# A two-block network on one core: the last expert tile added by one-hot products in PSUM, attention heads split from PSUM, one head scaled on GpSimd

## The chip, the cores and the metric

The kernel runs on one core of a Trainium2 chip. The metric is the device time of one execution in microseconds (us). Engines are named as the profile names them: PE is TensorE's matmul side and PEld its weight load, DVE is VectorE, ACT is ScalarE, POOL is GpSimd, and SP is SyncE, which here only starts transfers.

## The reference

One sequence of 512 tokens with 1024 channels goes through two layers of a first block (recurrence, latent attention, a convolutional feed-forward part) and then two layers of a second block. The change touches the second block alone. What it computes in each layer, cut to what matters:

```python
y_hy = hyena_mixer(...)                       # long convolution, here by DFT products
s = einsum(q, k); pr = softmax(s)             # 4 heads, two softmaxes each
o = einsum(pr[:, 0] - lam * pr[:, 1], v)
y_att = rms_norm_2(o, subln_g) * (1 - lam_init)
y_pool = pool_mixer(...)
h = layer_norm_2(ALPHA * h + concatenate([y_hy, y_att, y_pool]) @ w_out)
act = silu(h @ w1[e]) * (h @ w3[e]) * gate    # two of 16 experts for each token
y_moe = sum over e of act @ w2[e]
h = layer_norm_2(ALPHA * h + y_moe + y_ple)
```

## The kernel before

Activations are kept with channels on the 128 partitions and 512 tokens along the free axis, as 8 chunks. A large f32 product is made of three fp32r products, high by high, low by high and high by low (`three`, L257 to L259); so each operand is first split into a rounded high part and the rest. POOL splits the streamed weights (L180 makes the high part, L182 the low part), ACT and DVE split activations and the experts' weights.

The order of the work in the second block is written out by hand for each engine and held together by semaphores. Each engine runs its own list in order, so an instruction that waits holds up all that is behind it.

**The attention loop** has 16 steps n, four query blocks for each of four heads. In a step PE makes the scores for step n+2 (L2097), turns the weighted difference of the two softmaxes of step n (`turn`, L2110) and multiplies it with v (`weigh`, L2119). ACT takes the exponentials (L2450), copies the turned block (L2458) and scales the head's output (L2466). DVE takes the row maximum for step n+2 (L2777) and makes the difference for step n+1 (`difference`, L2784 to L2786). Between these, all three work on the hyena part: PE makes its projections and DFT products, ACT starts the short convolution of a tile (`hy_tile`, L2395), DVE ends it (`hy_taps`, L2666 and L2667), and `hyena_out` (L2826 on) writes the two output chunks at steps 13 and 14. Four blocks after a head began, DVE scales it by the reciprocal root (`norm_out`, L2806 and L2807, for heads 0, 1 and 2 at steps 4, 8 and 12), and PE turns it at steps 6, 10 and 14 (`turn_out`, L2127). At these steps DVE copies the turned head from PSUM to `tmp` (`att_take`, L2813), which sets `ot_taken`; PE's `turn` of steps 7, 11 and 15 waits for that, since both use PSUM bank 4. The split of `tmp` into `mix_h` and `mix_l` (L2641, L2642) comes at steps 7, 11 and 14. The last head is split from PSUM itself (L2875, L2876). POOL meanwhile forms the spectra's product, copies the inverse DFT's tables, and splits the first output weights, the third of them into a pair of buffers of its own (`split_apart`).

**The expert tiles** come after routing. There are 23 tiles of 128 rows: one for each expert, and 7 spare ones for experts with more than 128 tokens. POOL gathers a tile's rows by index (L1882). PE turns them (`turn_rows`, L2288) into two PSUM banks; ACT rounds them to `xgT_h` (L2575), DVE makes `xgT_l` (L3054). The expert's first weights, 2 MB, come in four parts, each rounded on ACT (L2569) and its rest taken on DVE (L3042). PE makes 24 products of 512 columns (`expert_up`, `ps<-ew_h,xgT_h` and its two like), ACT and DVE make the gated activation (L2597, L3097), PE turns it (L2326), DVE copies it (`hidden_evac`, L3060), and PE multiplies it by the 1 MB second weights (`expert_down`, L2344, plain f32). ACT and DVE each copy one half of the result (L2583, L3067), and POOL adds the rows to `yrows` in HBM by index (`scatter_rows`, L1913). DVE's list within a tile begins with the weights of the next one. For the first tile it is: three parts of tile 1's weights, a step of the residual (L3089), both halves of tile 1's rows, the activation, the fourth part.

**The end of a layer** starts when both of the last scatters have landed: SP loads `yrows` as four blocks of 128 tokens (L1792), PE has turned the residual z into the eight PSUM banks (L2364), DVE adds the two and sums each row (`pick_rows`, L3109), ACT squares (L2609), DVE and POOL normalise, and PE turns the four blocks back (L2373), once the last `pick_rows` has left the banks free. Scale and shift on ACT and DVE follow, and then the store or the next layer.

## Time and profile before

| what | value |
|---|---|
| runs | 2795.28, 2794.57 and 2798.91 us; median 2795.28 us |
| profiled execution | 2797.76 us, its span 2795.9 us |
| mean granted TensorE clock | 0.982 of full speed |
| PE busy | 2707.6 us, 97% of the span |
| DVE busy | 1746.7 us, 62% |
| POOL busy | 1601.3 us, 57% |
| ACT busy | 1096.7 us, 39% |

Times inside a run are us from the start of the span. The second block's layers have their attention loops at about 1740 to 1850 and 2310 to 2420, their expert tiles at 1956 to 2200 and 2527 to 2771, and their ends at 2200 to 2218 and 2771 to 2796. What stands in brackets behind a row, `[1.16 <-DVE tmp L2813]`, is the idle time of the engine just ahead of the row and what ended it.

### The profile page before, as it was taken

The numbers are of one execution on the slowest core, as the hardware profiler recorded it, in microseconds if no ns is written. First come the engines' busy times: TensorE is split into PE (matmuls) and PEld (weight loads), VectorE is DVE, ScalarE is ACT, GpSimd is POOL, SyncE is SP. The second block draws the span as 40 slices with busy tenths as digits, with TensorE's granted clock in tenths as the row PEclk, the third lists the DMA queues.
The fourth block names the chain that finished last, engine by engine and source line by source line (L and its number), as shares of the span: only waits on it lengthen the run. The fifth ranks groups of instructions, "written<-read, shape, count | busy, mean of one in ns | idle before, by whom it ended". The sixth has DMA issues, their size and how long they took to land. (4 is left out here: it accounts for less than half of the span.)

```text
span 2795.9 us, 35382 instructions
## 1 busy us (share of the span) xinstructions
PE 2707.6 (97%) x12410; PEld 2117.4 (76%) x12410; DVE 1746.7 (62%) x2544; ACT 1096.7 (39%) x1895; POOL 1601.3 (57%) x987
## 2 busy tenths in 40 slices
PE   8999999999999999999999999989999799899997
PEld 6777778888887777788888877778776577777775
DVE  6787755443137878654442148876877497877774
ACT  3744323222025544332221032544655315445553
POOL 5754466666677643476666765565236455662263
PEclk9999999999999999999999979999999999999999
DMA  4222222333332311223333322136995222257951
GB/s 153 83 76 61 63 88 76 98 98 98 95 94 79 96 61 61 68 80 96 96 98 106 97 74 91 54 106 230 336 353 160 82 88 69 91 202 288 347 173 61
DMA packets 89050, 337.16 MB, mean 121 GB/s; under 512 B 21584, under 2 KB 24400, under 8 KB 79568
## 3 DMA queue, kind: packets, MB, share of 16 engines
q1 hardware_dynamic: 66592, 298.02, 31.6%
q0 software_dynamic: 19296, 26.29, 3.6%
q10 hardware_dynamic: 3024, 11.01, 1.0%
q8 instruction: 87, 1.43, 0.2%
q14 instruction: 51, 0.42, 0.0%
HBM read 366.67 MB, written 34.60 MB: 144 GB/s over the span
## 5 line engine op out<-in xcount | busy, mean ns | idle before, releaser
L182 POOL TENSOR_TENSOR wl<-ring,wh 128x1024 fp32r<-128x1024 f32 x319 | 785.5, 2462 | 26.6
L180 POOL TENSOR_SCALAR wh<-ring 128x1024 fp32r<-128x1024 f32 x319 | 349.0, 1094 | 754.8 <-PE ps L259 529.3
L257 PE MATMUL ps<-xh,wh 128*128 128x512 f32 x1608 | 640.3, 398 | 15.3 <-DVE xl L1245 10.8
L258 PE MATMUL ps<-xl,wh 128*128 128x512 f32 x1608 | 628.6, 391 | 0.0
L259 PE MATMUL ps<-xh,wl 128*128 128x512 f32 x1608 | 628.5, 391 | 0.0
L257 PEld LDWEIGHTS ps<-xh,wh 128*128 128x128 f32 x1608 | 303.1, 189 | 96.0 <-issue 12.6
L259 PEld LDWEIGHTS ps<-xh,wl 128*128 128x128 f32 x1608 | 303.3, 189 | 64.6
L258 PEld LDWEIGHTS ps<-xl,wh 128*128 128x128 f32 x1608 | 303.5, 189 | 61.8 <-issue 1.0
L1487 DVE SCALAR_TENSOR_TENSOR taps<-ps,par,taps 128x511 f32<-128x511 f32 x192 | 143.8, 749 | 232.6 <-ACT taps L1219 217.7
L3042 DVE TENSOR_TENSOR ew_l<-ew,ew_h 128x1024 fp32r<-128x1024 f32 x184 | 213.3, 1217 | 4.4 <-ACT ew_h L2569 4.4
L2569 ACT ACTIVATE ew_h<-ew 128x1024 fp32r<-128x1024 f32 x184 | 180.4, 1050 | 10.6 <-DMA ew<-in_eu 7.2
L1219 ACT ACTIVATE taps<-ps,par 128x512 f32<-128x512 f32 x96 | 74.5, 778 | 271.8 <-PE ps L259 271.6
L2344 PE MATMUL ps<-ew,hactT 128*128 128x512 f32 x368 | 167.0, 597 | 4.4 <-DVE hactT L3060 4.4
L257 PE MATMUL ps<-ew_h,xgT_h 128*128 128x512 f32 x368 | 161.2, 438 | 4.6 <-issue 4.6
L379 DVE TENSOR_TENSOR z<-z,ps 128x512 f32<-128x512 f32 x44 | 30.2, 687 | 213.1 <-PE ps L259 212.7
L441 ACT ACTIVATE sqb<-z 128x512 f32<-128x512 f32 x48 | 30.3, 632 | 335.6 <-DVE z L379 247.4
L257 PE MATMUL ps<-hid_h,wh 128*128 128x512 f32 x384 | 149.9, 390 | 0.0
L259 PE MATMUL ps<-hid_h,wl 128*128 128x512 f32 x384 | 149.4, 389 | 0.0
L258 PE MATMUL ps<-hid_l,wh 128*128 128x512 f32 x384 | 149.4, 389 | 0.0
L259 PE MATMUL ps<-ew_h,xgT_l 128*128 128x512 f32 x368 | 144.8, 393 | 0.0
L258 PE MATMUL ps<-ew_l,xgT_h 128*128 128x512 f32 x368 | 144.5, 393 | 0.0
L1882 POOL DMA_INDIRECT xg<-xrows,idx x46 | 48.3, 1050 | 138.7 <-PE ps L2288 122.7
(537 smaller groups left out, 5329.1 us busy)
## 6 DMA issues: line engine op xcount, KB each, us to landing
ring<-in_w SPq DMA_DIRECT2D x343, 512.0 KB, 3.6
ew<-in_eu SPq DMA_DIRECT2D x32, 2048.0 KB, 11.4
ew<-in_ed SPq DMA_DIRECT2D x32, 1024.0 KB, 11.9
xrows<-xr ACTq DMA_DIRECT2D x8, 512.0 KB, 2.7
yrows<-xr ACTq DMA_DIRECT2D x8, 512.0 KB, 3.6
yg<-yrows SPq DMA_DIRECT2D x8, 512.0 KB, 5.1
z<-in_x SPq DMA_DIRECT2D x4, 512.0 KB, 6.0
out<-z SPq DMA_DIRECT2D x8, 256.0 KB, 2.9
```

The source lines that it names most:

```text
L180: nc.gpsimd.tensor_scalar(hi, raw, 1.0, 0.0, ALU.mult, ALU.add).then_inc(sem["w_hi"], 1)
L182: nc.gpsimd.tensor_tensor(lo, raw, hi, ALU.subtract).then_inc(sem["w_split"], 1)
L257: nc.tensor.matmul(out, wh, xh, start=first, stop=False, **kw)
L258: nc.tensor.matmul(out, wh, xl, start=False, stop=False, **kw)
L259: return nc.tensor.matmul(out, wl, xh, start=False, stop=last, **kw)
L441: nc.scalar.activation(sqb[:, m % 2, :], z[:, m, :], ACT.Square).then_inc(sem["sq_part"], 1)
L1219: nc.scalar.activation(taps[:, j % 2, half, :], ps[:, 2 * j + half, :], ACT.Identity, scale=col(layer, "ffw", f + (2 * 2 * FC + half * FC) ...
L1487: ins = V.scalar_tensor_tensor(out, ps[:, 2 * j + half, 0:S - s], col(layer, "ffw", f + ((2 - s) * 2 * FC + half * FC)), out, ALU.mult, AL ...
L1882: nc.gpsimd.indirect_dma_start(xg[:, j % 2, :], None, xrows[:, :], bass.IndirectOffsetOnAxis(ap=idx[:, held(j):held(j) + 1], axis=0), boun ...
L2344: mm = T.matmul(ps[:, 5 + half, :], hactT[:, f, :], ew[:, b, a_:a_ + S], start=(f == 0), stop=(f == EC - 1))
L2569: A(ew_h[:, n % HI_SLOTS, :], ew[:, b, u * D:u * D + D], ACT.Copy).then_inc(sem["e_hi"], 1)
L3042: V.tensor_tensor(ew_l[:, b, u * D:u * D + D], ew[:, b, u * D:u * D + D], ew_h[:, n % HI_SLOTS, :], ALU.subtract).then_inc(sem["e_lo"], 1)
```

## The change

In the attention loop `att_take` now writes `mix_h` and `mix_l` straight from PSUM (two instructions on DVE where there were one at this place and two later), the buffer `tmp` and the semaphore `ot_taken` are gone, and PE's `turn` of steps 7, 11 and 15 waits for `att_done`. The scaling of head 2 goes from DVE to POOL, ahead of its split of the first output weights; DVE keeps the reciprocal and signals `o_root`. POOL's `split_apart` waits until the 16th difference is made. ACT starts the last hyena tile ahead of the exponentials of step 13 and not behind them.

Around the first expert tiles, ACT brings the table for the Silu up front and rounds the second half of tile 1's rows before tile 0's activation. DVE takes the two halves of tile 1's rows between the parts of tile 1's weights.

At a layer's end, tile 22 is no longer scattered. The SP loads wait for the 22 other scatters only. DVE keeps the last tile's row indices, turns them into four one-hot matrices `last_hot` (128 by 512 in all) at tile 8, and ACT and DVE split the last tile's result into `last_h` and `last_l`. PE turns z with matmuls that leave the PSUM groups open and adds `last_hot` by `last_h` and by `last_l` in each of the eight banks: 16 fp32r products of 512 columns more in each layer.

```diff
+        last_hot = at_("last_hot", 180, [P, 4, P], F32R)
+        last_h = at_("last_h", 164, [P, D], F32R)
+        last_l = at_("last_l", 176, [P, D], F32R)
...
+        TAP_LAST = 11
         HALF_AT = {7: (4, 0), 8: (4, 1), 9: (5, 0), 10: (5, 1)}
         FOLD_AT = 8
+        POOL_HEAD = 2
         NORM_AT = (2,)
         STACK_AT = 1
-        SPLIT_AT = (7, 11, 14)
...
-                    sp.wait_ge(sem["y_out0"], at("y_out0", 16 * turns_of(TILES, 0, 2)))
-                    sp.wait_ge(sem["y_out1"], at("y_out1", 16 * turns_of(TILES, 1, 2)))
+                    sp.wait_ge(sem["y_out0"], at("y_out0", 16 * turns_of(TILES - 1, 0, 2)))
+                    sp.wait_ge(sem["y_out1"], at("y_out1", 16 * turns_of(TILES - 1, 1, 2)))
...
+                    g.wait_ge(sem["o_root"], at("o_root", 1))
+                    nc.gpsimd.tensor_tensor(osb[:, POOL_HEAD % 2, :, :], osb[:, POOL_HEAD % 2, :, :],
+                                            headv[:, POOL_HEAD % 2, 4:8].unsqueeze(2).to_broadcast([P, 4, P]), ALU.mult
+                                            ).then_inc(sem["o_nrm"], 1)
                     split_one(g, nc, sem, sh, u0 + V_OUT, at("unit_done", SPLIT + V_IDFT + 2))
                     split_one(g, nc, sem, sh, u0 + V_OUT + 1, at("unit_done", SPLIT + V_OUT))
+                    g.wait_ge(sem["a_ready2"], at("a_ready2", 4 * AHEADS))
                     split_apart(g, nc, sem, sh, u0 + V_OUT + SPLIT, apart_out)
...
-                    scatter_rows(TILES - 1)
...
                         if n >= 7 and n % 4 == 3:
-                            pe.wait_ge(sem["ot_taken"], at("ot_taken", (n - 3) // 4))
+                            pe.wait_ge(sem["att_done"], at("att_done", (n - 3) // 4))
...
+                    def turn_tokens(c):
+                        for k in range(C8):
+                            T.matmul(ps[:, 2 * c + k // 4, k % 4 * P:k % 4 * P + P], z[:, k, c * P:c * P + P], ident, is_transpose=True,
+                                     start=k % 4 == 0, stop=False, skip_group_check=True)
+                    def add_last(c, half):
+                        cols = slice(half * S, half * S + S)
+                        T.matmul(ps[:, 2 * c + half, :], last_hot[:, c, :], last_h[:, cols], start=False, stop=False, skip_group_check=True)
+                        mm = T.matmul(ps[:, 2 * c + half, :], last_hot[:, c, :], last_l[:, cols], start=False, stop=True, skip_group_check=True)
+                        if half:
+                            mm.then_inc(sem["zt_mm"], 1)
                     turn_hidden(TILES - 1)
+                    turn_tokens(0)
                     expert_down(TILES - 1)
-
-                    for c in range(4):
-                        if c == 2:
-                            pe.wait_ge(sem["y_lo"], at("y_lo", TILES))
-                        if c == 3:
-                            pe.wait_ge(sem["y_hi"], at("y_hi", TILES))
-                        for k in range(C8):
-                            mm = T.transpose(ps[:, 2 * c + k // 4, k % 4 * P:k % 4 * P + P], z[:, k, c * P:c * P + P], ident)
-                        mm.then_inc(sem["zt_mm"], 1)
+                    pe.wait_ge(sem["y_lo"], at("y_lo", TILES))
+                    add_last(0, 0)
+                    turn_tokens(1)
+                    pe.wait_ge(sem["y_hi"], at("y_hi", TILES))
+                    add_last(0, 1)
+                    add_last(1, 0)
+                    add_last(1, 1)
+                    for c in (2, 3):
+                        turn_tokens(c)
+                        add_last(c, 0)
+                        add_last(c, 1)
...
+                        if n == TAP_LAST:
+                            hy_tile(TAP_AT[n])
                         if n + 2 < 4 * AHEADS:
                             expo(n + 2)
-                        if n in TAP_AT:
+                        if n in TAP_AT and n != TAP_LAST:
...
+                            A(eps[:, 2:3], eps[:, 0:1], ACT.Silu)
                             act.wait_ge(sem["up_mm"], at("up_mm", UP_PARTS // 2))
                             turn_evac(1, (0,))
                         act.wait_ge(sem["up_mm"], at("up_mm", UP_PARTS * (j + 1)))
+                        if j == 0:
+                            turn_evac(1, (1,))
                         if j:
                             act.wait_ge(sem["hact"], at("hact", j))
                         A(sil[:, :], ps[:, 2 + j % 2, 0:DE], ACT.Silu).then_inc(sem["silu"], 1)
-                        if j + 1 < TILES:
-                            turn_evac(j + 1, (0, 1) if j else (1,))
+                        if j and j + 1 < TILES:
+                            turn_evac(j + 1)
...
-                    y_evac(TILES - 1)
+                    for half, done in enumerate(("dn_half", "dn_mm")):
+                        act.wait_ge(sem[done], at(done, TILES))
+                        A(last_h[:, half * S:half * S + S], ps[:, 5 + half, :], ACT.Copy).then_inc(sem["y_high"], 1)
...
+                        ins = V.reciprocal(headv[:, h % 2, 4:8], headv[:, h % 2, 4:8])
+                        if h == POOL_HEAD:
+                            ins.then_inc(sem["o_root"], 1)
+                            return
...
-                        V.tensor_scalar(tmp[:, h % 2, :], ps[:, 4, :], lamt[:, 5:6], None, ALU.mult).then_inc(sem["ot_taken"], 1)
-
-                    def att_split(h):
-                        dve.wait_ge(sem["ot_taken"], at("ot_taken", h + 1))
-                        split(tmp[:, h % 2, :], mix_h[:, HYC + h, :], mix_l[:, HYC + h, :], "att_done")
+                        do(V.tensor_scalar(mix_h[:, HYC + h, :], ps[:, 4, :], lamt[:, 5:6], None, ALU.mult))
+                        V.scalar_tensor_tensor(mix_l[:, HYC + h, :], ps[:, 4, :], lamt[:, 5:6], mix_h[:, HYC + h, :], ALU.mult, ALU.subtract
+                                               ).then_inc(sem["att_done"], 1)
...
-                        if n in SPLIT_AT:
-                            att_split(SPLIT_AT.index(n))
                     norm_out(AHEADS - 1)
-                    dve.wait_ge(sem["ot_mm"], at("ot_mm", AHEADS))
-                    do(V.tensor_scalar(mix_h[:, HYC + AHEADS - 1, :], ps[:, 4, :], lamt[:, 5:6], None, ALU.mult))
-                    V.scalar_tensor_tensor(mix_l[:, HYC + AHEADS - 1, :], ps[:, 4, :], lamt[:, 5:6], mix_h[:, HYC + AHEADS - 1, :],
-                                           ALU.mult, ALU.subtract).then_inc(sem["att_done"], 1)
+                    att_take(AHEADS - 1)
...
+                    last_row = wrap[:, TILES - 1:TILES]
+                    dve.wait_ge(sem["idx_ready"], at("idx_ready", 2))
+                    do(V.scalar_tensor_tensor(last_row, last_row, float(NOWHERE), ps[:, 6, TILES - 1:TILES], ALU.add, ALU.add))
+                    def spread_last():
+                        do(V.tensor_tensor(wrap[:, 0:4], last_row.to_broadcast([P, 4]), con_rt("tile", 4), ALU.subtract))
+                        do(V.tensor_tensor(last_hot[:, :, :], con_rt("iota").unsqueeze(1).to_broadcast([P, 4, P]),
+                                           wrap[:, 0:4].unsqueeze(2).to_broadcast([P, 4, P]), ALU.is_equal))
+                    def turn_evac(j, halves=(0, 1)):
+                        for half in halves:
...
-                        if j + 1 < TILES:
+                        if j == 0:
+                            weights_low(1, (0,))
+                            turn_evac(1, (0,))
+                            weights_low(1, (1,))
+                            turn_evac(1, (1,))
+                            weights_low(1, (2,))
+                        elif j + 1 < TILES:
                             weights_low(j + 1, range(UP_PARTS - 1))
+                        if j == C8:
+                            spread_last()
...
-                        if j + 1 < TILES:
+                        if j and j + 1 < TILES:
...
-                    y_evac(TILES - 1)
+                    for half, done in enumerate(("y_lo", "y_hi")):
+                        cols = slice(half * S, half * S + S)
+                        dve.wait_ge(sem["y_high"], at("y_high", half + 1))
+                        V.tensor_tensor(last_l[:, cols], ps[:, 5 + half, :], last_h[:, cols], ALU.subtract).then_inc(sem[done], 1)
```

On DVE the attention loop reads as follows from the 13th step's row maximum to the next but one (`hy` is the hyena tile, `pexp` the exponentials, `osb` a head's output, `headv` its roots, `small` the row maxima). Before:

```order
L2777 TENSOR_REDUCE small_11943<-ps 128x2
L2666 SCALAR_TENSOR_TENSOR hy<-ps,par_55,hy 128x511
L2667 SCALAR_TENSOR_TENSOR hy<-ps,par_55,hy 128x511
L2641 TENSOR_SCALAR mix_h<-tmp_11940 128x512
L2642 TENSOR_TENSOR mix_l<-tmp_11940,mix_h 128x512
L2784 RECIPROCAL headv<-small_11943 128x2
L2785 TENSOR_SCALAR small_11943<-headv,small_11943,lamt 128x1
L2786 SCALAR_TENSOR_TENSOR pexp<-pexp,small_11943 128x512
L2777 TENSOR_REDUCE small_11943<-ps 128x2
L2806 RECIPROCAL headv<-headv 128x4
L2807 TENSOR_TENSOR osb_11857<-osb_11857,headv 128x512
```

Now:

```order
L2809 TENSOR_REDUCE small_11946<-ps 128x2
L2698 SCALAR_TENSOR_TENSOR hy<-ps,par_55,hy 128x511
L2699 SCALAR_TENSOR_TENSOR hy<-ps,par_55,hy 128x511
L2816 RECIPROCAL headv<-small_11946 128x2
L2817 TENSOR_SCALAR small_11946<-headv,small_11946,lamt 128x1
L2818 SCALAR_TENSOR_TENSOR pexp<-pexp,small_11946 128x512
L2809 TENSOR_REDUCE small_11946<-ps 128x2
L2838 RECIPROCAL headv<-headv 128x4
```

The two split instructions and the multiplication of `osb` have left this place; the split stands a step earlier, as the two instructions that read PSUM.

On PE the end of a layer's tiles reads as follows (`hact` and `hactT` are the activation and its transpose, `cst` holds the identity). Before:

```order
L2326 MATMUL ps<-cst_11941,hact 128x128 x2
L2344 MATMUL ps<-ew,hactT 128x512 x4
L2326 MATMUL ps<-cst_11941,hact 128x128 x2
L2344 MATMUL ps<-ew,hactT 128x512 x4
L2364 MATMUL ps<-cst_11941,z 128x128 x32
L2373 MATMUL ps<-cst_11941,yg 128x128 x32
```

Now, up to the second block of tokens:

```order
L2334 MATMUL ps<-cst_11944,hact 128x128 x2
L2366 MATMUL ps<-cst_11944,z 128x128 x8
L2352 MATMUL ps<-ew,hactT 128x512 x4
L2372 MATMUL ps<-last_h,last_hot 128x512
L2373 MATMUL ps<-last_l,last_hot 128x512
L2366 MATMUL ps<-cst_11944,z 128x128 x8
L2372 MATMUL ps<-last_h,last_hot 128x512
L2373 MATMUL ps<-last_l,last_hot 128x512
```

Eight of the 32 transposes of z stand ahead of the last `expert_down`, and the products follow it, four for each block of tokens.

On DVE the first expert tile reads as follows from tile 1's weights on. Before:

```order
L3042 TENSOR_TENSOR ew_l<-ew,ew_h 128x1024 x4
L3089 SCALAR_TENSOR_TENSOR z<-z,spec 128x512
L3054 TENSOR_TENSOR xgT_l<-ps,xgT_h 128x512 x2
L3097 SCALAR_TENSOR_TENSOR hact<-sil,slot_gate,ps 128x256
L3042 TENSOR_TENSOR ew_l<-ew,ew_h 128x1024 x4
```

Now:

```order
L3071 TENSOR_TENSOR ew_l<-ew,ew_h 128x1024 x2
L3093 TENSOR_TENSOR xgT_l<-ps,xgT_h 128x512
L3071 TENSOR_TENSOR ew_l<-ew,ew_h 128x1024
L3093 TENSOR_TENSOR xgT_l<-ps,xgT_h 128x512
L3071 TENSOR_TENSOR ew_l<-ew,ew_h 128x1024
L3136 SCALAR_TENSOR_TENSOR z<-z,spec 128x512
L3144 SCALAR_TENSOR_TENSOR hact<-sil,slot_gate,ps 128x256
L3071 TENSOR_TENSOR ew_l<-ew,ew_h 128x1024 x4
```

Of each listed group of weight parts, the first or last belongs to the neighbouring tile. What moved are the two halves of the rows, from behind three parts and the residual to behind the first and the second part.

## Rows read from the trace of the kernel before

**Rows 1.** Waits of PE, first layer's attention: total us, times, longest us.

```profile
PE ps L2110 <- DVE tmp L2813: 2.0, 2, 1.2
...
PE ps L257 <- ACT pexp L2450: 1.6, 1, 1.6
...
PE ps L257 <- DVE hy L2667: 1.2, 1, 1.2
```

**Rows 2.** Timeline, first attention loop: start, us, engine, line, tiles [idle before].

```profile
1808.01 1.30 POOL L1822 TENSOR_TENSOR yfull<-spec 128x512 f32<-128x512 f32 x1
...
1825.11 0.78 ACT L2395 ACTIVATE hy<-ps,par 128x512 f32<-128x512 f32 x1
...
1825.92 0.75 DVE L2666 SCALAR_TENSOR_TENSOR hy<-ps,par,hy 128x511 f32<-128x511 f32 x1 [2.18 <-ACT hy L2395]
...
1830.67 2.40 POOL L182 TENSOR_TENSOR wl<-ring,wh 128x1024 fp32r<-128x1024 f32 x1
...
1830.94 2.68 DVE L2807 TENSOR_TENSOR osb<-osb,headv 128x512 f32<-128x512 f32 x1
...
1834.71 1.22 DVE L2777 TENSOR_REDUCE small<-ps 128x2 f32<-128x1024 f32 x1
...
1839.28 2.38 POOL L182 TENSOR_TENSOR apart_ol<-ring,apart_oh 128x1024 fp32r<-128x1024 f32 x1
...
1839.32 2.88 DVE L2786 SCALAR_TENSOR_TENSOR pexp<-pexp,small 128x512 f32<-128x512 f32 x1
...
1843.01 0.63 PE L2110 MATMUL ps<-cst,pexp 128*128 128x128 f32 x4 [1.16 <-DVE tmp L2813]
```

**Rows 3.** Timeline, second layer's first expert tiles.

```profile
2541.75 0.47 PE L257 MATMUL ps<-ew_h,xgT_h 128*128 128x512 f32 x1 [2.30 <-issue]
...
2544.20 2.96 ACT L2569 ACTIVATE ew_h<-ew 128x1024 fp32r<-128x1024 f32 x3 [2.90 <-DMA ew<-in_eu]
...
2545.30 3.50 DVE L3042 TENSOR_TENSOR ew_l<-ew,ew_h 128x1024 fp32r<-128x1024 f32 x3 [1.53 <-ACT ew_h L2569]
...
2549.91 3.70 PE L2344 MATMUL ps<-ew,hactT 128*128 128x512 f32 x8 [1.33 <-DVE hactT L3060]
```

**Rows 4.** Timeline, end of the second layer.

```profile
2765.43 3.70 PE L2344 MATMUL ps<-ew,hactT 128*128 128x512 f32 x8 [0.90 <-DVE hactT L3060]
...
2765.85 1.55 POOL L1913 DMA_INDIRECT yrows<-y_b,idx  x1 [8.17 <-DVE y_b L3067]
...
2767.45 0.60 ACT L2583 ACTIVATE y_a<-ps 128x512 f32<-128x512 f32 x1 [4.22 <-PE ps L2344]
...
2768.96 3.66 PE L2364 MATMUL ps<-cst,z 128*128 128x128 f32 x32
...
2770.66 1.55 POOL L1913 DMA_INDIRECT yrows<-y_a,idx  x1 [3.26 <-DVE y_a L3067]
...
2773.40 1.75 SPq L1792 DMA_DIRECT2D yg<-yrows  x4
...
2776.79 1.22 DVE L3109 SCALAR_TENSOR_TENSOR yg<-yg,ps 128x1024 f32<-128x1024 f32 x1 [6.93 <-DMA yg<-yrows]
...
2781.72 1.20 DVE L3109 SCALAR_TENSOR_TENSOR yg<-yg,ps 128x1024 f32<-128x1024 f32 x1
...
2782.99 5.32 PE L2373 MATMUL ps<-cst,yg 128*128 128x128 f32 x32 [10.37 <-DVE yg L3109]
```

**Rows 5.** Timeline, end of the first layer.

```profile
2202.57 1.75 SPq L1792 DMA_DIRECT2D yg<-yrows  x4
```

**Rows 6.** Chain in order of time, one fp32r product: start, us, what.

```profile
2757.60 0.23 PE ps L259
```

**Rows 7.** Window: length, PE, PEld, DVE, ACT, POOL busy, PEclk, DMA, GB/s.

```profile
2784.00:2785.00 1.00, 1.00 (x7) 1.00 (x6) 0.16 (x1) 0.77 (x3) 0.83 (x1) 0.50 0.03 8
```

**Rows 8.** First layer's first expert tiles: the same for a window, then a timeline row.

```profile
1970.00:1972.00 2.00, 1.77 (x5) 1.47 (x6) 2.00 (x4) 0.00 (x0) 0.00 (x0) 0.63 0.96 410
...
1978.46 3.60 PE L2344 MATMUL ps<-ew,hactT 128*128 128x512 f32 x8
```

18 lines of the change are left out of this document (8 added, 10 removed).

## The prediction

> **What bounds the kernel now.** I read the page first: PE is busy for 97% of the span, no other engine for more than 62%. Time can only come out of the places where PE waits, and I looked for these with the waits and the timeline of three places, all in the second block, each of which occurs in two layers. In the attention loop PE waits for DVE and ACT in single steps: twice for the copy of a turned head, once for exponentials, once for the last hyena tile [rows 1]. The rows to read there are DVE's [rows 2]: it is occupied from 1825.92 on, and two of its instructions take 2.68 and 2.88 us. Each overlaps a POOL subtraction of two tiles (2.40 and 2.38 us) and ends 0.54 to 0.55 us after POOL's (1833.62 against 1833.07, 1842.20 against 1841.66). Both read two tiles in SBUF. At the first expert tiles PE stands for 2.30 us before tile 1, and in the second layer for another 1.33 us before the first `expert_down` [rows 3]. At a layer's end it stands for 10.37 us [rows 4]: the last scatter is issued at 2770.66, the loads follow at 2773.40, the first sum at 2776.79, the last at 2781.72, and only behind that do the transposes begin.
>
> **The end of a layer** carries the largest term. The scatter of tile 21 is issued at 2765.85, that of tile 22 at 2770.66, and SP's loads leave 2.74 us after the latter [rows 4]. The former has the same form and nothing ahead of it that is late, so I give it the same 2.74 us: loads at 2768.59, 4.81 us sooner. If the loads take what they took, the four sums start 4.81 us sooner too, the first at 2771.98 and the last at 2776.91. In the first layer the loads left at 2202.57 [rows 5], 2.74 us behind a scatter likewise.
>
> The new work must hide beneath these loads. Eight transposes of z come to 0.92 us (3.66 for 32) and fit into the 0.9 us in which PE waited for the last hidden tile, ahead of 2765.43. `expert_down` ends as before at about 2769.1. ACT rounds the first half at 2767.45 for 0.60 us, as it copied it, and DVE's subtraction from PSUM takes about 0.7 us; the second half is so rounded and split by about 2770.5. An fp32r product takes 0.23 us from the one before it [rows 6]. PE has then made the first product pair and eight transposes; it makes six products (1.4 us) by 2771.9, and two further blocks, each 0.92 us of transposes and four products at 0.92, by 2775.6. The sums of blocks 2 and 3 need theirs by 2775.5 (behind the third load) and 2776.9, against 2773.8 and 2775.6: the 16 products, 3.7 us a layer, cost nothing, with 1.3 us to spare at the last. So the term is **-4.8 us a layer, -9.6 us**. Were the cover gone, each us beyond 1.3 would be lost.
>
> Behind the last sum 32 transposes take 5.32 us, where 32 of the same shape took 3.66 [rows 4]. The granted clock was still at the lower level there, after the idle 10.37 us (0.50, which is 1.2 GHz, in the window from 2784 [rows 7]). With PE at work to 2775.6, the idle time shrinks to some 2.5 us. If the clock stays up this gives nearly the 1.66 us between the two, 1.5 a layer, if not nothing. I take nothing, and keep 1.5 for the range, for the reason below.
>
> **Attention.** In each layer ACT's start of the last hyena tile (1825.11) moves ahead of the exponentials; DVE waited for it for 2.18 us, so its pair begins at 1823.7 [rows 2], and PE's 1.2 us wait for that tile goes [rows 1]. The split of head 1 (two instructions, about 1.1 us) leaves step 11; its price at step 10 is one more PSUM instruction, 0.75 us as the pair's, in a place where DVE then idles for the next exponentials anyway. The 2.68 us scaling leaves DVE. What is late next is POOL. It now multiplies for 1.30 us, the row of a like product, from about 1828.2, and its split of the first output weights, which waited for the inverse DFT, starts at 1829.5 as before. Hence its subtraction still ends at about 1833.1, and now it is DVE's difference of step 14 that is held, to 1833.6. The last row maximum follows there and not at 1834.71: 1.1 us won of nearly 6 us freed. From that row maximum to PE's turn at 1843.01 took 8.3 us. Of this 2.1 go, since the last difference no longer meets a POOL subtraction (2.88 against 0.75; `split_apart` waits for it), and 0.8 come, the second instruction that reads PSUM before PE may turn. PE's own list ahead of the turn gives some 0.3 us back. The turn comes at about 1840.8, 2.2 us sooner, and all behind it, the last head above all, shifts with it: **-4.3 us in two layers**. The bounds are 0, should POOL hold DVE for as long as before, and the three PE waits behind 1825, 1.2, 1.6 and 1.2 us [rows 1]: -4.0 us a layer. `split_apart` ends a us later than before, 10 us ahead of its use.
>
> Moving an elementwise product to POOL has a price: 1.30 us there [rows 2]. The Trainium skill speaks against it (GPSIMD Engine Reference, Key points): VectorE is about twice as fast at elementwise work, and GpSimd shares its SBUF interfaces with VectorE instructions that have two SBUF inputs. The held rows agree with the second half; by that rule alone the move would lose DVE the whole 1.30 us, and the sum would be 2.6 us worse.
>
> **First expert tiles.** By the order, DVE has the first half of tile 1's rows ready while PE still works at tile 0, and the second in time; PE can go on at once, and the 2.30 us wait goes. But what ends the next wait is the load of tile 2's weights. It lands at 2544.20, ACT rounds three parts (2.96 us), DVE's rest ends at 2548.8, then a residual step and the copy of the hidden tile: PE's `expert_down` at 2549.91 is released by that [rows 3]. The load's own trigger, the end of the early projection, is not touched. So in the second layer the 2.30 us become a longer wait before 2549.91: gain 0. In the first layer PE came to its `expert_down` at 1978.46 with no wait shown [rows 8], slowed by a low clock, and DVE's chain was ready just before: -0.2 us. Bounds: nothing, and 2.30 us a layer. The one-hot matrices cost DVE some 0.8 us at tile 8, beside PE's tile time; I put 0.1 us a layer for it, 0.8 at worst. The Silu's table load only changes place in time that ACT had free.
>
> **The sum.** -9.6 - 4.3 - 0.2 + 0.2 = -13.9 us. The profiled execution took 2797.76 us (span 2795.9) and would take 2783.9. It lies 2.5 us above the median of the runs, 2795.28, from which I get **2781.4 us**.
>
> **The rivals.** *The clock falls at the new gaps.* PE's wait before the first `expert_down` grows to about 3 us. After a wait of 2.30 us the clock fell in the first layer (0.63 over 1970 to 1972 [rows 8]), where the load hid it, and did not in the second. A fall costs what it cost the 32 transposes, 1.66 us [rows 4]. Twice that behind the new gaps, where nothing hides it, gives 2784.7 us. Its opposite is a clock that stays up there and at both ends: -3.0, 2778.4 us. The Trainium skill (TensorE: Matmul & The Clock Gate, HAM oscillation) says that waits between bursts bring the low rate back; that is for the first of these, and the second layer's gap here speaks against taking it as certain.
>
> *Attention gives nothing*, because POOL's shifted split holds a DVE instruction on the path: 2785.7 us. For it, that both long instructions were held; against it, that `split_apart` now waits.
>
> *The rows at tile 1 do what they seem to*: the 2.30 us are won in both layers, with a load that lands in time: 4.4 us more, 2777.0 us. The ACT row that waits 2.90 us for the load speaks against it.
>
> *The products run at the plain f32 rate.* Their place is the layer's end. `expert_down`, plain f32, takes 3.60 us for four products of 512 columns (the row counts each twice) [rows 8], 0.90 each against 0.23. With 14 of the 16 behind the first transposes of block 1, PE would end at 2786.1, 4.4 us behind the old last sum (2781.72) where I forecast 4.8 ahead. That takes 9.2 us a layer: 2795.28 - 13.9 + 18.4 = 2799.8 us, slower than before. It decides from about 0.75 us a product on. All three tiles are declared fp32r, as those of [rows 6], so I hold it unlikely. The Trainium skill (FP8 and Floating Point Precision, TensorE Precision Notes) counts four passes for true FP32; at four times [rows 6] this is 0.92 us.
>
> **How the numbers follow.** Forecast, 2779.5 to 2783.5: 0.55. Clock down: 0.12. Clock up: 0.12. Attention nothing: 0.11. Rows at tile 1 won: 0.05. Products slow: 0.05. The range from 2777.0 to 2786.5 takes in the first five with the bounds of the terms above, and leaves out the last and what two of them give together. 0.2% is 5.6 us, about what can be told from no change: faster needs less than 2789.7 us, which all but the last case give, 0.93 with something kept for a cause I have not seen; the last lies within the bound or just beyond: same 0.04, slower 0.03.
>
> **What would show it.** Right: SP's loads right behind tile 21's scatter and the first sum some 4.8 us nearer to the last tile; PE's turn of step 15 some 2.2 us nearer to the loop's start; a wait of about 3 us before the first `expert_down` that ends with DVE's copy; product steps of 0.23 us. Wrong: a sum that waits for PE, a difference stretched past POOL's end at step 15, a first `expert_down` that starts 2 us sooner, or a low clock behind it.

## The result and the profile after

The changed kernel took 2780.07 us (median of 4 runs, 2779.15 to 2785.5), the kernel before beside it 2796.91 us (4 runs). The ratio is 0.9941, with a 95% interval of 0.993 to 0.9953: 0.6% faster. The forecast was 2781.4 us, with a range from 2777.0 to 2786.5. The profiled execution took 2780.18 us, 17.6 less than that of before, where the sum gave 13.9.

The page of the changed kernel, its span and its first part:

```profile
span 2778.4 us, 35448 instructions
...
PE 2714.0 (98%) x12442; PEld 2120.3 (76%) x12442; DVE 1741.6 (63%) x2544; ACT 1098.2 (40%) x1899; POOL 1598.2 (58%) x987
```

PE is busy for 6 us more than before in a span 17.5 us shorter: the change took out waiting, not work. (There are 32 more products, at 0.23 us each.) To see where, cut the second block of both traces at the same PE instructions (in the timeline): attention is from the first turn of exponentials to the turn of step 15, "first tiles" from the first expert product to the first `expert_down`, "tiles" from there to the last `expert_down`, "end" from there to the final transposes, "tail" from those of the second layer to the end of the span.

| us, first and second layer | before | changed | difference | forecast |
|---|---|---|---|---|
| attention | 92.13, 93.71 | 89.27, 90.30 | -2.86, -3.41 | -2.15 each |
| attention to first tiles | 119.31, 119.57 | 119.50, 119.34 | +0.19, -0.23 | 0 |
| first tiles | 16.14, 16.06 | 15.85, 15.88 | -0.29, -0.18 | -0.2, 0 |
| tiles | 216.13, 215.52 | 216.52, 215.77 | +0.39, +0.25 | +0.1 each |
| end | 18.42, 17.56 | 13.16, 12.53 | -5.26, -5.03 | -4.8 each |
| final transposes to next attention; tail | 107.56; 12.91 | 107.62; 11.67 | +0.06; -1.24 | 0 |

These differences and 0.1 us ahead of the first turn sum to the 17.5 us of the spans.

**End of a layer.** Timeline of the changed kernel, end of the second layer, then one row of the first layer:

```profile
2754.62 1.55 POOL L1922 DMA_INDIRECT yrows<-y_b,idx  x1 [8.16 <-DVE y_b L3106]
...
2757.38 1.75 SPq L1796 DMA_DIRECT2D yg<-yrows  x4
...
2758.56 0.69 DVE L3154 TENSOR_TENSOR last_l<-ps,last_h 128x512 fp32r<-128x512 f32 x1 [1.03 <-ACT last_h L2636]
...
2760.75 1.22 DVE L3159 SCALAR_TENSOR_TENSOR yg<-yg,ps 128x1024 f32<-128x1024 f32 x1 [1.50 <-DMA yg<-yrows]
...
2764.17 0.39 PE L2373 MATMUL ps<-last_l,last_hot 128*128 128x512 f32 x1
...
2765.47 1.20 DVE L3159 SCALAR_TENSOR_TENSOR yg<-yg,ps 128x1024 f32<-128x1024 f32 x1
...
2766.73 4.01 PE L2398 MATMUL ps<-cst,yg 128*128 128x128 f32 x32 [2.18 <-DVE yg L3159]
...
2205.29 5.38 PE L2398 MATMUL ps<-cst,yg 128*128 128x128 f32 x32 [2.81 <-DVE yg L3159]
```

The loads follow tile 21's scatter by 2.76 us (forecast 2.74 [rows 4]), the first sum is released by its load and not by PE, and PE starts its last product 1.3 us ahead of the last sum. Counted from the product's end, 0.23 us later, as the forecast counted, PE is 1.1 us ahead where 1.3 were forecast. PE's idle 10.37 us [rows 4] have shrunk to 2.18. In the second layer the 32 transposes then took 4.01 us, in the first still 5.38. Two windows of the changed kernel, columns as in [rows 7], show why:

```profile
2206.00:2208.00 2.00, 2.00 (x11) 2.00 (x10) 0.91 (x2) 0.99 (x3) 0.79 (x1) 0.50 0.83 338
2767.00:2769.00 2.00, 2.00 (x19) 1.83 (x18) 0.55 (x3) 1.51 (x4) 1.20 (x1) 1.00 0.02 4
```

The granted clock was 0.50 behind the idle 2.81 us and 1.00 behind the idle 2.18 us. That is the 1.24 us in the tail. It is not a sure gain: in ten profiles with this code at the end (the changed kernel's and nine of the experiments below), the clock stayed up behind the second layer's wait in seven and fell in three, behind waits of 1.98 to 2.80 us. Behind the first layer's, 2.57 to 4.33 us, it stayed up in one.

**Attention.** First layer of the changed kernel, timeline; the counterparts are in [rows 2]:

```profile
1823.05 0.73 DVE L2698 SCALAR_TENSOR_TENSOR hy<-ps,par,hy 128x511 f32<-128x511 f32 x1
...
1824.90 1.05 POOL L243 TENSOR_SCALAR wl<-ring 128x1024 fp32r<-128x1024 f32 x1
...
1825.15 1.34 DVE L2818 SCALAR_TENSOR_TENSOR pexp<-pexp,small 128x512 f32<-128x512 f32 x1
...
1827.79 1.04 POOL L1866 TENSOR_TENSOR osb<-osb,headv 128x512 f32<-128x512 f32 x1 [1.84 <-DVE headv L2838]
...
1829.93 2.40 POOL L182 TENSOR_TENSOR wl<-ring,wh 128x1024 fp32r<-128x1024 f32 x1
...
1830.61 2.28 DVE L2818 SCALAR_TENSOR_TENSOR pexp<-pexp,small 128x512 f32<-128x512 f32 x1
...
1832.81 1.21 DVE L2809 TENSOR_REDUCE small<-ps 128x2 f32<-128x1024 f32 x1
...
1837.41 0.75 DVE L2818 SCALAR_TENSOR_TENSOR pexp<-pexp,small 128x512 f32<-128x512 f32 x1
...
1839.36 0.75 DVE L2850 SCALAR_TENSOR_TENSOR mix_l<-ps,lamt,mix_h 128x512 fp32r<-128x512 f32 x1
...
1840.26 0.63 PE L2118 MATMUL ps<-cst,pexp 128*128 128x128 f32 x4 [0.33 <-DVE mix_l L2850]
```

The difference of step 14 starts inside POOL's subtraction and ends 0.56 us behind it (1832.89 against 1832.33). The last difference takes 0.75 us, not 2.88. The turn comes at 1840.26, not 1843.01.

**First tiles.** Second layer of the changed kernel, timeline:

```profile
2533.82 3.50 DVE L3071 TENSOR_TENSOR ew_l<-ew,ew_h 128x1024 fp32r<-128x1024 f32 x3 [0.92 <-ACT ew_h L2596]
...
2537.95 0.42 DVE L3099 COPY hactT<-ps 128x256 f32<-128x256 f32 x1
...
2538.43 3.70 PE L2352 MATMUL ps<-ew,hactT 128*128 128x512 f32 x8 [2.73 <-DVE hactT L3099]
```

The wait ahead of tile 1 is gone and stands ahead of the first `expert_down`, 2.73 us long (2.70 in the first layer). The stretch is hardly shorter.

### The profile page after: what moved, and what is told of

Its sections match the earlier page's. It is cut to its first block and busy times, and to the rows that moved or that the text cites. A ratio compares the mean times of both kernels' runs of the same rounds, so it can differ in the third digit from the quotient of the medians.

```text
span 2778.4 us, 35448 instructions
## 1 busy us (share of the span) xinstructions
PE 2714.0 (98%) x12442; PEld 2120.3 (76%) x12442; DVE 1741.6 (63%) x2544; ACT 1098.2 (40%) x1899; POOL 1598.2 (58%) x987
## 5 line engine op out<-in xcount | busy, mean ns | idle before, releaser
L180 POOL TENSOR_SCALAR wh<-ring 128x1024 fp32r<-128x1024 f32 x319 | 349.4, 1095 | 742.9 <-PE ps L259 521.9
## 6 DMA issues: line engine op xcount, KB each, us to landing
ew<-in_ed SPq DMA_DIRECT2D x32, 1024.0 KB, 10.9
```

Of the source, the lines that this page charges most:

```text
L180: nc.gpsimd.tensor_scalar(hi, raw, 1.0, 0.0, ALU.mult, ALU.add).then_inc(sem["w_hi"], 1)
```

## Experiments

All are edits of the changed kernel. The table has the stretches of each profile, cut as above (first layer, second layer), and the median of all its runs. Attention is given for the first layer, since in the second the granted clock fell for a few us somewhere in the loop of every profile but that of `hidden_sooner`.

| | attention | first tiles | tiles | end | tail | median us (runs) |
|---|---|---|---|---|---|---|
| before | 92.13 | 16.14, 16.06 | 216.13, 215.52 | 18.42, 17.56 | 12.91 | 2796.91 (4) |
| changed | 89.27 | 15.85, 15.88 | 216.52, 215.77 | 13.16, 12.53 | 11.67 | 2780.07 (4) |
| end_undone | 89.34 | 15.88, 15.96 | 216.48, 217.22 | 18.11, 17.20 | 14.09 | 2794.57 (11) |
| att_undone | 92.12 | 16.14, 15.96 | 216.36, 217.46 | 13.09, 12.73 | 11.64 | 2786.76 (5) |
| tiles_undone | 89.36 | 15.82, 16.18 | 216.61, 215.77 | 13.36, 13.10 | 13.00 | 2780.14 (5) |
| head_on_dve | 88.19 | 16.30, 16.37 | 219.87, 217.49 | 14.16, 12.37 | 11.51 | 2779.35 (5) |
| split_early | 89.35 | 16.01, 15.92 | 216.41, 215.78 | 13.78, 13.03 | 11.63 | 2782.9 (4) |
| tap_late | 88.99 | 16.36, 16.01 | 218.28, 215.79 | 13.78, 12.72 | 11.69 | 2780.78 (4) |
| products_twice | 89.31 | 16.29, 15.94 | 218.56, 215.76 | 15.01, 15.01 | 11.54 | 2785.74 (4) |
| psum_undone | 88.55 | 16.19, 16.16 | 216.94, 217.50 | 13.58, 12.38 | 11.56 | 2779.6 (4) |
| psum_alone | 89.78 | 15.95, 16.08 | 217.98, 217.43 | 14.41, 13.17 | 11.61 | 2784.66 (4) |
| turn_sooner | 89.35 | 16.15, 16.20 | 217.95, 217.45 | 11.06, 11.11 | 13.09 | 2782.35 (4) |
| hidden_sooner | 89.32 | 13.07, 13.12 | 217.80, 216.46 | 12.91, 12.36 | 13.07 | 2775.71 (4) |
| both | 88.23 | 13.02, 13.03 | 218.16, 216.45 | 14.69, 12.55 | 13.06 | 2777.05 (5) |

Runs of one kernel lie up to 10 us apart, so for a part worth a microsecond the stretch decides: with the attention code unchanged, six profiles give 89.27 to 89.36 us. The kernel before, run beside each group of experiments, had medians from 2796.42 to 2798.22 us, so medians of two groups differ by 1 or 2 us for no reason of their own.

**The three parts taken back, one at a time.**

`end_undone` has the lines of before for the layer's end:

```diff
+                    scatter_rows(TILES - 1)
...
-                    pe.wait_ge(sem["y_lo"], at("y_lo", TILES))
-                    add_last(0, 0)
-                    turn_tokens(1)
...
+                    y_evac(TILES - 1)
```

`att_undone` takes back all four edits of the attention loop at once, which stand one by one below. `tiles_undone`:

```diff
-                            A(eps[:, 2:3], eps[:, 0:1], ACT.Silu)
...
-                        if j == 0:
-                            weights_low(1, (0,))
-                            turn_evac(1, (0,))
...
-                        elif j + 1 < TILES:
+                        if j + 1 < TILES:
```

> The changed kernel with its end-of-layer part taken back: tile 22 is scattered again, no one-hot products. Against the changed kernel, whose trace gives from the last expert_down to the final transposes 13.16 and 12.53 us (18.42 and 17.56 before) and whose second final transposes ran at the full clock. Theory (the parts add up, the end of a layer is worth 10.3 us in those two stretches, another 1.2 us by the clock behind the second, and 0.6 us is paid back at the tiles): 2780.1 + 10.9 = 2791.0 us. Rival (the clock gain is not this part's, the 1.2 us stay): 2789.8 us. Rival (the products and matrices cost more than the tiles show): below 2788 us.

> The changed kernel with the whole attention part taken back: split of heads 0 to 2 by way of tmp, head 2 scaled on DVE, last hyena tile behind the exponentials, no wait ahead of split_apart. By the two traces the turn of step 15 comes 2.86 and 3.41 us sooner after the first turn. Theory (the parts add up): 2780.1 + 6.3 = 2786.4 us, with PE's 1.2 us wait for the last hyena tile back. Rival (the prediction's price of 2.15 us a layer was right and the rest came from elsewhere): 2784.4 us.

> The changed kernel with the first tiles' part taken back: tile 1's rows in the order of before, no table load up front. Theory (the load of tile 2's weights limits, so the 2.3 us wait ahead of tile 1 comes back and the 2.7 us wait ahead of the first expert_down shrinks by as much): 2780.5 us, at most 0.6 us above the changed kernel. Rival (the clock drops in one wait and not in the other, as in the first layer of before): the same time within 0.6 us but a granted clock of 0.50 in the first layer behind the wait. Rival (the rows' order is worth its wait): 2784.7 us.

The end is worth 4.95 and 4.67 us in its own stretch. The median of `end_undone` lies 14.5 us above the changed kernel's, more than the 10.9 worked out; its profiled execution lies 12.3 us above. The stretches that are longer beside the end's own show the clock at work. Behind the idle 10.92 and 10.00 us the final transposes took 6.67 and 6.47 us, so that the next stretch was longer by 1.34 us in the first layer (108.96 us to the next attention) and by 2.42 in the second (tail), and the clock fell behind the second layer's 2.81 us wait ahead of `expert_down` (second tiles, 1.45 us more). The remaining stretches together were 2.5 us shorter. The kernel before, with idle times of 11.23 and 10.37 us, needed 5.30 and 5.32 us for the same transposes, so the longer low clock does not follow from the idle time, and the surplus is not a price of this part. Attention is worth 2.85 us in the first layer and 6.7 us in the medians, as expected. The first tiles' part is worth nothing: 2780.14 us without it. PE's wait ahead of tile 1 came back at 2.31 us in both layers, and the one ahead of the first `expert_down` shrank to 1.09 and 1.47.

**The four edits in attention.** Three were taken back alone, then the fourth, then all but the fourth.

`head_on_dve`, `split_early`, `tap_late` and `psum_undone`, in this order; `psum_alone` is the first three together:

```diff
-                    g.wait_ge(sem["o_root"], at("o_root", 1))
-                    nc.gpsimd.tensor_tensor(osb[:, POOL_HEAD % 2, :, :], osb[:, POOL_HEAD % 2, :, :],
...
```

```diff
-                    g.wait_ge(sem["a_ready2"], at("a_ready2", 4 * AHEADS))
```

```diff
-                        if n == TAP_LAST:
-                            hy_tile(TAP_AT[n])
...
-                        if n in TAP_AT and n != TAP_LAST:
+                        if n in TAP_AT:
```

```diff
-                        do(V.tensor_scalar(mix_h[:, HYC + h, :], ps[:, 4, :], lamt[:, 5:6], None, ALU.mult))
+                        V.tensor_scalar(tmp[:, h % 2, :], ps[:, 4, :], lamt[:, 5:6], None, ALU.mult).then_inc(sem["ot_taken"], 1)
...
+                        if n in SPLIT_AT:
+                            att_split(SPLIT_AT.index(n))
```

> The changed kernel with head 2 scaled on DVE again and nothing else. In the changed kernel's trace POOL multiplies from 1827.79 to 1828.83 and its subtraction of the first output weights runs from 1829.93 to 1832.33; DVE's difference of step 14 starts at 1830.61 and ends 0.56 us behind that subtraction, at 1832.89. Theory (with the hyena tile sooner the head's scaling falls ahead of the subtraction; on DVE it takes 0.7 us in time that DVE has free, POOL's subtraction starts 1.1 to 1.3 us sooner, and the difference ends as much sooner): -1.2 us a layer, 2777.7 us. Rival (the move to POOL is worth what it took from DVE before, the scaling is held by POOL for 2.7 us again): +2 us a layer, 2784 us. Rival (something else ends the wait): 2780.1 us.

> The changed kernel without POOL's wait for the 16th difference ahead of split_apart. The attention stretch (first turn to turn 15) was 89.27 and 90.30 us in the changed kernel. Theory A, the prediction's (the wait keeps POOL's subtraction off the last difference and wins 2.1 us a layer): 91.3 and 92.4 us, 2784.3 us. Theory B (whichever of the two starts first holds the interface; with all else 2 us sooner, DVE's difference at 1837.4 starts ahead of POOL's subtraction, which now comes at 1837.7, and is held only by the rest of POOL's one-input instruction, 0.1 us): 89.4 and 90.4 us, 2780.3 us.

> The changed kernel with the last hyena tile behind the exponentials again. Theory (DVE's pair waits for ACT's start and pushes the difference of step 13 and the row maximum behind it by about 2 us, some of which is taken up by the wait for exponentials): attention stretch 90.5 to 91.5 us in the first layer, 2782.5 to 2784.5 us. Rival (the row maximum of step 15 hangs on POOL's subtraction alone, which starts by PE's inverse DFT): 89.3 us, 2780 us.

> The changed kernel with heads 0 to 2 copied to tmp and split later again; the head on POOL, the hyena tile ahead and the wait before split_apart stay. Attention stretch of the changed kernel 89.27 and 90.30 us, of before 92.13 and 93.71. Theory A, from the prediction's sums (two instructions ahead of the turn cost 0.8 us, the split at step 11 saved 1.1 us): 89.0 to 89.8 us in the first layer, 2780 us. Theory B (none of the other three parts was worth anything when it was taken back alone, so the split from PSUM carries the whole): 92 us, 2786 us.

> The changed kernel with only the split from PSUM left of the attention part: head 2 on DVE, the last hyena tile behind the exponentials, no wait before split_apart. Theory B (the split from PSUM carries the whole, and POOL's multiplication only delays its subtraction): 88.0 to 89.3 us in the first layer, 2778 to 2780 us. Theory C (the parts stand in for each other: each takes DVE's two-input instructions out of POOL's subtractions, and any of them does; with all three gone DVE meets both subtractions again, 2.7 and 2.9 us): 91.0 to 92.1 us, 2784 to 2786 us.

None of the four, taken back alone, gives back any of the 2.86 us: 88.19, 89.35, 88.99 and 88.55 us. (The median of `split_early`, 2782.9 us, lies 2.8 above the changed kernel's, nearer to theory A's time than to B's; but A puts the loss into attention, and there is none there.) With only the PSUM split left, 89.78: 2.35 of the 2.86. That is between theories B and C. B is out, since `psum_undone` is faster than the changed kernel; C is right in its idea (the edits stand in for each other) and wrong in its number: in `psum_alone` the head's scaling starts at 1829.73, ahead of POOL's subtraction at 1830.38, and takes 1.10 us, and the last difference takes 1.44, where C had 2.7 and 2.9. The rows of DVE and POOL show the idea. In `head_on_dve`, `split_early`, `tap_late` and, from two engine lists, `psum_undone`:

```profile
1828.98 1.21 DVE L2834 TENSOR_TENSOR osb<-osb,headv 128x512 f32<-128x512 f32 x1
...
1829.73 2.71 POOL L182 TENSOR_TENSOR wl<-ring,wh 128x1024 fp32r<-128x1024 f32 x1
...
1831.86 1.13 DVE L2813 SCALAR_TENSOR_TENSOR pexp<-pexp,small 128x512 f32<-128x512 f32 x1
```

```profile
1839.56 0.75 DVE L2817 SCALAR_TENSOR_TENSOR pexp<-pexp,small 128x512 f32<-128x512 f32 x1
...
1839.85 2.72 POOL L182 TENSOR_TENSOR apart_ol<-ring,apart_oh 128x1024 fp32r<-128x1024 f32 x1
```

```profile
1832.17 0.75 DVE L2815 SCALAR_TENSOR_TENSOR pexp<-pexp,small 128x512 f32<-128x512 f32 x1
...
1832.35 2.83 POOL L182 TENSOR_TENSOR wl<-ring,wh 128x1024 fp32r<-128x1024 f32 x1
```

```profile
1833.12 0.75 DVE L2819 SCALAR_TENSOR_TENSOR pexp<-pexp,small 128x512 f32<-128x512 f32 x1
...
1833.40 2.71 POOL L182 TENSOR_TENSOR wl<-ring,wh 128x1024 fp32r<-128x1024 f32 x1
```

Where DVE's difference starts first, it takes its 0.75 us and POOL's subtraction is stretched from 2.38 or 2.40 to 2.71 or more. Where POOL's starts first, DVE's lasts until 0.55 us behind it. Some 0.3 us of start time decide over 1.5 to 2.1 us. In `tap_late` and `psum_undone` DVE is late, and POOL is late by more: its multiplication waits for DVE's reciprocal (L2838 in the changed kernel). Counted from the first turn, the reciprocal and with it POOL's subtraction come 1.6 and 2.1 us later than in the changed kernel, and the difference of step 14, which waits for ACT's exponentials, only 0.7 and 1.1. So it meets POOL from the front: no loss. In `head_on_dve` POOL's subtraction is not delayed by its own multiplication. It ends at 1832.44, 80.27 us behind the first turn, where the changed kernel's ends 81.34 us behind it, and the difference is held for 0.4 us only: 1.08 us won. The head itself took 1.21 us on DVE, held by POOL's rounding (L180, 1828.61 to 1829.65), where the same instruction takes 0.69 us at step 4. The second layer can't confirm it: its loop took 89.19 us, but 89.32 to 90.99 in the six profiles with the attention code unchanged, by where the clock was low. The medians show only 0.7 us of this: in the profiled execution the clock fell behind both waits at the first tiles, and the third sum at the first layer's end waited 1.83 us for its load, not 0.40.

**The cover of the products.** The cover is the time by which PE is done with the products before the loads would have let the last sum start. Here each pair of products is made twice (and the last tile is so added twice):

```diff
+                        T.matmul(ps[:, 2 * c + half, :], last_hot[:, c, :], last_l[:, cols], start=False, stop=False, skip_group_check=True)
+                        T.matmul(ps[:, 2 * c + half, :], last_hot[:, c, :], last_h[:, cols], start=False, stop=False, skip_group_check=True)
```

> The changed kernel with each pair of one-hot products made twice: 16 fp32r products more in each layer, 0.23 us each, 3.7 us; the last tile is added twice. In the changed kernel's trace PE ends the last product at 2764.40 and DVE starts the last sum at 2765.47. Theory (the cover is 1.1 us, as worked out: 1.3): from the last expert_down to the final transposes 13.16 and 12.53 become 15.8 and 15.1 us, and with PE's idle stretch cut short the clock stays up behind both: 2780.1 + 5.2 - 1.5 = 2783.8 us, 2785.3 us if it falls. Rival (the loads set the pace whatever PE does): 2780 us.

The ends became 15.01 us both, 1.85 and 2.48 more for 3.7 us of products: the cover is 1.9 us in the first layer and 1.2 in the second, where 1.1 was expected for both. The first layer's is larger because the changed kernel's last two sums had waited 0.40 and 0.27 us for their loads there. Now PE's product releases the last sum (timeline of `products_twice`):

```profile
2772.24 0.39 PE L2375 MATMUL ps<-last_l,last_hot 128*128 128x512 f32 x1
...
2772.67 1.22 DVE L3161 SCALAR_TENSOR_TENSOR yg<-yg,ps 128x1024 f32<-128x1024 f32 x1 [1.21 <-PE ps L2375]
```

The stretch from the first layer's final transposes on was 106.18 us for 107.62: there the clock did not fall. PE's idle time ahead of the second layer's transposes was 1.32 us, and behind it they took 3.93. The median, 2785.74 us, is 1.9 above the theory's 2783.8.

**The wait ahead of the first `expert_down`.**

```diff
+                        elif j == 1:
+                            weights_low(2, (0,))
+                            hidden_evac(0)
+                            weights_low(2, (1, 2))
```

> The changed kernel with DVE's copy of tile 0's hidden activation moved from behind three parts of tile 2's weights and a residual to behind the first part. In the changed kernel PE waits 2.70 and 2.73 us for that copy (1975.61, 2538.43), while tile 0's expert_down needs nothing of tile 2. Theory (the copy only stands in line behind the loaded weights; expert_down(0) can start at once and fills the gap, and the next tile's products start when the rows' second part is done, some 1.4 us sooner; no idle stretch is left in which the clock could fall): up to the first expert_down 13.2 us for 15.9, the rest of the tiles 1.3 longer for it, -1.4 us a layer, 2777.3 us, and runs that lie closer together. Rival (the load of tile 2's weights limits all that follows, so the wait only moves to tile 2's first products): 2780.1 us. Rival (the delayed weights make tile 2 late): up to 2782 us.

Timeline of `hidden_sooner`, second layer:

```profile
2531.63 0.42 DVE L3099 COPY hactT<-ps 128x256 f32<-128x256 f32 x1
...
2532.11 3.70 PE L2352 MATMUL ps<-ew,hactT 128*128 128x512 f32 x8
```

First tiles and tiles together: 230.87 and 229.58 us for 232.37 and 231.65, 1.5 and 2.1 us won, as the theory had it. The median, 2775.71 us, lies 4.4 us below the changed kernel's, 3.6 of which these stretches show. At the layers' ends the clock gave and took: it stayed up behind PE's 2.57 us wait in the first (106.23 us to the next attention, not 107.62) and fell behind the 1.98 us in the second (tail 13.07, not 11.67).

**The clock behind that wait.** Windows behind the first `expert_down`, of the changed kernel, `head_on_dve` and `att_undone`, two each (first and second layer):

```profile
1976.00:1978.00 2.00, 2.00 (x6) 0.90 (x5) 1.14 (x3) 0.37 (x1) 0.00 (x0) 1.00 0.96 410
2540.00:2542.00 2.00, 2.00 (x6) 0.80 (x6) 0.00 (x0) 1.55 (x3) 0.00 (x0) 1.00 0.99 422
```

```profile
1976.00:1978.00 2.00, 2.00 (x3) 0.97 (x4) 1.34 (x3) 0.00 (x0) 0.00 (x0) 0.50 0.94 401
2542.00:2544.00 2.00, 2.00 (x4) 0.97 (x3) 0.76 (x2) 0.00 (x0) 0.00 (x0) 0.50 0.95 406
```

```profile
1980.00:1982.00 2.00, 1.92 (x5) 0.96 (x6) 1.61 (x4) 0.00 (x0) 0.00 (x0) 1.00 1.05 451
2546.00:2548.00 2.00, 2.00 (x4) 0.84 (x3) 0.00 (x1) 0.23 (x1) 0.00 (x0) 0.50 0.98 420
```

The waits were 2.70 and 2.73, 3.14 and 3.22, and 2.99 and 2.81 us: behind 2.99 us the clock stayed at the upper level, behind 2.81 it went to the lower one. Of the ten profiles that have this wait in one piece (the changed kernel's and those of all experiments but `tiles_undone`, `hidden_sooner` and `both`), 11 of 20 waits were followed by a low clock. The tiles behind it then took 217.2 to 217.5 us in the second layer, and else 215.76 to 215.79: 1.7 us. In the first layer they took 217.95 to 218.56, once 219.87, and else 216.36 to 216.94. In the three kernels without the long wait it did not fall there in any of six places, though `tiles_undone` has its 2.31 us ahead of tile 1. In the kernel before, the clock fell behind such a 2.30 us in one layer of two.

**The final transposes begun sooner.**

```diff
-                    pe.wait_ge(sem["zt_taken"], at("zt_taken", 4))
                     for c in range(4):
...
-                        for i, k in enumerate(LAST_FIRST):
+                        for i, k in enumerate(SOONER if c == 0 else LAST_FIRST):
+                            if c == 0 and i in SOONER_TAKEN:
+                                pe.wait_ge(sem["zt_taken"], at("zt_taken", SOONER_TAKEN[i]))
```

> The changed kernel with the final transposes of the first block of tokens put into banks as the sums leave them (four behind the second sum, two behind the third, two behind the fourth) and not all behind the fourth. In the changed kernel PE idles 2.81 and 2.18 us ahead of these transposes, which then take 5.4 us at a granted clock of 0.50 in the first layer. Theory (PE is not idle for more than some 1.1 us at a time, so the clock stays up, and behind the last norm only eight transposes are left): the first layer's end 1.5 us shorter, the second's 0.2 us: 2778.4 us, the granted clock 1.00 behind both. Rival (the clock falls all the same): 2779.3 us. Rival (the early transposes hold up the last products' sums): 2781 us.

Timeline and three windows of `turn_sooner`, first layer:

```profile
2204.17 0.66 PE L2400 MATMUL ps<-cst,yg 128*128 128x128 f32 x4 [0.65 <-POOL yg L1949]
...
2209.08 3.18 PE L2400 MATMUL ps<-cst,yg 128*128 128x128 f32 x16 [0.43 <-POOL yg L1949]
```

```profile
2204.00:2206.00 2.00, 0.86 (x6) 0.62 (x6) 1.46 (x5) 0.11 (x2) 0.11 (x1) 1.00 1.05 414
2206.00:2208.00 2.00, 1.05 (x10) 0.82 (x9) 1.44 (x4) 1.97 (x4) 1.37 (x2) 1.00 1.01 412
2208.00:2210.00 2.00, 1.57 (x10) 1.18 (x9) 0.94 (x2) 0.96 (x3) 1.02 (x1) 0.55 0.76 311
```

No single wait of PE was over 1 us, and the clock fell all the same, behind 4 us in which PE worked about half the time (0.86 and 1.05 of 2.00). With the transposes begun earlier, end and what follows must be taken together: 121.44 us for 120.78 in the first layer, 24.20 for 24.20 in the second. Nothing is won; the first theory is out, since it had the clock at 1.00 behind both ends. What the edit gives when the clock stays up is not shown by the first layer, where the third sum also waited longer for its load (1.70 us for 0.40); in the second the clock was 1.00 with and without it, and the two are equal.

**Both edits that shortened a stretch.**

> The changed kernel with the two edits that shortened a stretch: head 2 scaled on DVE (attention stretch 88.19 us for 89.27) and the copy of tile 0's hidden activation behind the first part of tile 2's weights (first tiles and the tiles behind them 1.5 and 2.1 us shorter together). They lie 100 us apart. Theory (they add): attention 88.2 us, up to the first expert_down 13.1 us in both layers, 2775.7 - 2.2 = 2773.5 us. Rival (with the tiles sooner the load at the layer's end lands no sooner and takes the gain back): 2775.7 us.

Attention took 88.23 us and the first tiles 13.02 and 13.03: the two stretches add as expected. The time does not show it: 2773.5 us was expected. In the profiled execution the loss stands at the first layer's end, where DVE's third sum waited 2.20 us for its load, not 0.34 as in `hidden_sooner` (timelines of `both` and of `hidden_sooner`):

```profile
2202.70 1.22 DVE L3154 SCALAR_TENSOR_TENSOR yg<-yg,ps 128x1024 f32<-128x1024 f32 x1 [2.20 <-DMA yg<-yrows]
```

```profile
2200.88 1.22 DVE L3163 SCALAR_TENSOR_TENSOR yg<-yg,ps 128x1024 f32<-128x1024 f32 x1 [0.34 <-DMA yg<-yrows]
```

The end took 14.69 us for 12.91, and behind PE's 4.33 us wait the clock was low: 108.37 us to the next attention for 106.23. That is 3.9 us, more than the head's scaling wins. The third sum waited about as long in `head_on_dve`, `psum_alone` and `turn_sooner` (1.83, 2.05 and 1.70 us). Why the load comes late no run shows, so the rival, that the loads at the end take the gain back, is not excluded. The median was 2777.05 us, the fastest run 2772.78, the fastest of all kernels. Against the kernel before the ratios are 0.9924 (0.991 to 0.9938) for `both` and 0.9926 (0.9909 to 0.9942) for `hidden_sooner`. Both beat the kernel before. Their medians lie 3.0 and 4.4 us below the changed kernel's, with intervals that still overlap its own (0.993 to 0.9953); which of the two is faster stays open.

## Why the prediction was right, and where not

- **End of a layer, -9.6 us.** Right by its own steps: 2.76 us from scatter to loads, sums released by the loads, 0.23 us a product, the last cover 1.1 us for 1.3. Measured -10.29 us, and taking the part back alone gave 9.62 in the same stretches.
- **The clock behind it.** The 1.5 us a layer kept for the range came in the second layer (1.24) and not in the first. It was not part of the sum, and by the other profiles it is a matter of chance.
- **Attention, -4.3 us; measured -6.27.** The path was the right one: turn(15) by way of the last row maximum, that by a difference held by POOL. One term, the start of POOL's subtraction, was mis-sized, for two reasons. It was taken to start where it had before, to end at 1833.1; it ended at 1832.33. The multiplication took 1.04 us for 1.30, and the split that PE's inverse DFT releases was ready sooner, for which PE's vanished 1.2 us wait is the likely cause. So the row maximum came at 1832.81 for 1833.6. From it to the turn it took 7.45 us, for 7.2 forecast (before: 8.30).
- **What each edit is worth.** Here the prediction's reasons fail. It gave 2.1 us a layer to the wait ahead of `split_apart`; without the wait nothing changed, because with all else 2 us sooner the last difference starts ahead of POOL's subtraction anyway. It took the head on POOL as a help with a price hidden in POOL's free time; it costs 1.1 us, measured in the first layer. The sentence from the Trainium skill (GPSIMD Engine Reference, Key points) that spoke against this move had the sign right: by it the sum would have been 2.6 us worse, and the measured price is 2.2 us if the second layer is like the first, which no run pins down. It came by another way: POOL's multiplication, from 1827.79 to 1828.83, held no instruction of DVE, which was idle, but it delayed POOL's subtraction, and that one held DVE's difference. What the prediction lacked stands in the Trainium skill under SBUF — State Buffer, "SBUF: two separate sides": the shared pair of ports is an exclusive lock that goes to whichever starts first. The rows above agree, POOL's 2.71 us included.
- **First tiles, -0.2 us; measured -0.47.** The wait moved, at the length forecast (about 3 us; 2.70 and 2.73). The reason was half right. The load of tile 2's weights did end the wait, but only because the copy stood behind them in DVE's list; `expert_down` of tile 0 needs nothing of tile 2, and with the copy ahead 1.5 to 2.1 us are won.
- **One-hot matrices and tiles, +0.2 us; measured +0.64.** Within the 0.8 a layer given as the worst.
- **The rivals.** The clock that falls at the new gaps got 0.12. In the profiled execution it did not fall there, in 11 of 20 like waits it did, for about 1.7 us each: it belonged into the sum at about half its price, and it may account for part of the spread of the runs (2779 to 2785 us), which no trace of the slower ones shows. Slow products: 0.23 us each, out. Rows at tile 1 won: out. Attention gives nothing: out.

Between the medians the change gave 16.8 us where the sum had 13.9. The forecast time is only 1.3 us off because the median of before, measured beside it, was 1.6 us higher than the one shown.

## What to carry to other kernels

When two engines share a path and an edit shifts one by a microsecond, price the meeting and not the edit: look for who starts first, and expect edits that avoid the same meeting not to add. Before a wait is put down to a load, ask whether the waiting instruction needs what was loaded or only stands behind it in its engine's list; moving it is then a one-line change. And a PE wait of about 3 us should be carried with the chance of a clock drop behind it: here 11 of 20 waits of 2.70 to 3.22 us, at about 1.7 us each.

## What the runs showed of the hardware

- POOL and DVE hold each other, and either can be first. DVE's instruction with two inputs in SBUF ended 0.54 to 0.56 us behind POOL's; POOL's subtraction grew from 2.38 or 2.40 to 2.71 to 2.83 us behind DVE's start. A POOL instruction with a single input in SBUF holds DVE too: L243 from 1824.90 to 1825.95, and the difference from 1825.15 ended at 1826.49 (rows of the changed kernel above).
- The granted clock after a PE wait is not a function of the wait's length at this resolution: 1.00 behind 2.99 us, 0.50 behind 2.81, 0.55 in a stretch whose single waits were all under 1 us but in which PE worked half the time. At a layer's end it stayed at 1.00 behind 2.57 us in the first layer of `hidden_sooner` and fell behind 1.98 us in the second.
- How long the clock stays low also varies: 32 transposes behind an idle 11.23 us took 5.30 us in the kernel before, and behind 10.92 us 6.67 in `end_undone`.
